# A decoder layer's tail: the last two gate tiles passed over by token halves, the sample rows turned at once

## What is computed

```
e = _rmsnorm(p_l @ w_ple, g_ple)
h = h + jax.nn.sigmoid(h @ w_ple_gate) * e
...
return _rmsnorm(h, g_final), jnp.stack(S_out), jnp.stack(buf_out)
```

## Time and profile before

| | us |
|---|---|
| timed runs, median of 3 (lowest, highest) | 1185.35 (1182.74, 1187.15) |
| the profiled execution, whole | 1180.84 |
| its span, first to last instruction | 1178.8 |
| mean granted TensorE clock in it | 0.995 of full |

### The profile page before, as it was taken

One profiled execution on the slowest core, in us unless ns is written; L12 is line 12 of the kernel. 1 busy time (PEld: TensorE's weight loads), 2 busy tenths in 40 slices (PEclk: granted clock), 3 DMA queues, 4 the chain that ended last, 5 costly groups with the idle time before them and its releaser, 6 DMA issues.

```text
span 1178.8 us, 30314 instructions
## 1 busy us (share of the span) xinstructions
PE 1163.9 (99%) x12182; PEld 1038.8 (88%) x12182; DVE 978.5 (83%) x1509; ACT 562.6 (48%) x804; POOL 55.5 (5%) x80
## 2 busy tenths in 40 slices
PE   9999999999999999999999999999999999999996
PEld 7888888888888899899998999999889999999885
DVE  6688599678867898998989989788897888887686
ACT  6445645555446744444434444444444444445442
POOL 2122210100000200000000000000000000000000
PEclk9999999999999999999999999999999999999998
DMA  7776775765566566666666666666666666667552
GB/s 257 242 231 178 233 213 180 226 181 189 175 219 197 179 213 198 201 193 201 205 212 196 195 199 195 213 208 196 196 209 189 206 205 198 196 197 249 166 158 74
DMA packets 193112, 234.89 MB, mean 199 GB/s; under 512 B 7987, under 2 KB 153626, under 8 KB 192761
## 3 DMA queue, kind: packets, MB, share of 16 engines
q1 hardware_dynamic: 187568, 220.29, 59.4%
q0 software_dynamic: 3968, 11.89, 3.5%
q10 hardware_dynamic: 1504, 1.70, 0.4%
HBM read 226.89 MB, written 7.43 MB: 199 GB/s over the span
## 4 chain that ended last, share of the span: by engine, by line
PE 90%; DVE 6%; ACT 2%; issue 1%; DMA 1%; ACTq 0%; SPq 0%; DVEq 0%
PE acc L2210 13%; PE acc L1816 10%; PE acc L1820 10%; PE acc L1818 10%; PE acc L2246 7%; PE acc L2212 6%; PE acc L2213 6%; PE acc L2191 5%; PE acc L2193 5%; PE wrk L2191 4%; PE wrk L2193 4%; PE acc L2248 4%; PE acc L2249 4%; DVE hl L952 2%; ACT hl L592 1%
## 5 line engine op out<-in xcount | busy, mean ns | idle before, releaser
L952 DVE SCALAR_TENSOR_TENSOR hl<-raw,hl 128x1024 f16<-128x1024 f32 x414 | 494.4, 1220 | 67.2 <-ACT hl L592 64.0
L592 ACT ACTIVATE hl<-raw 128x1024 f16<-128x1024 f32 x414 | 421.7, 1051 | 173.9 <-DMA raw<-in_w_down_dram 86.1
L2210 PE MATMUL acc<-nrm,hl 128*128 128x264 f16 x1344 | 274.8, 276 | 0.0
L1818 PE MATMUL acc<-nrm,hl 128*128 128x264 f16 x952 | 262.8, 276 | 0.0
L1820 PE MATMUL acc<-nrm,hl 128*128 128x264 f16 x952 | 262.7, 276 | 0.0
L1816 PE MATMUL acc<-nrm,hl 128*128 128x264 f16 x952 | 262.7, 276 | 0.0
L2212 PE MATMUL acc<-nrm,hl 128*128 128x264 f16 x672 | 185.5, 276 | 0.0
L2213 PE MATMUL acc<-nrm,hl 128*128 128x264 f16 x672 | 185.5, 276 | 0.0
L2246 PE MATMUL acc<-big,hl 128*128 128x264 f16 x704 | 146.2, 276 | 0.0
L2210 PEld LDWEIGHTS acc<-nrm,hl 128*128 128x128 f16 x1344 | 128.9, 98 | 17.8 <-DVE tg L1434 0.2
L1816 PEld LDWEIGHTS acc<-nrm,hl 128*128 128x128 f16 x952 | 93.3, 98 | 13.5 <-issue 0.4
(11 more groups left out here) (425 smaller groups left out, 2050.8 us busy)
## 6 DMA issues: line engine op xcount, KB each, us to landing
raw<-in_w_gate_up_dram SPq DMA_DIRECT2D x168, 512.0 KB, 4.6
raw<-in_w_down_dram SPq DMA_DIRECT2D x88, 512.0 KB, 4.8
raw<-in_w_in_dram SPq DMA_DIRECT2D x80, 512.0 KB, 4.4
raw<-in_w_out_dram SPq DMA_DIRECT2D x32, 512.0 KB, 4.8
raw<-in_w_ple_gate_dram SPq DMA_DIRECT2D x32, 512.0 KB, 5.2
state<-in_state_hgrn_dram POOLq DMA_DIRECT2D x8, 512.0 KB, 5.9
out_new_hgrn_sample_dram<-state POOLq DMA_DIRECT2D x8, 512.0 KB, 5.1
raw<-in_w_gate_up_dram SPq DMA_DIRECT2D x16, 256.0 KB, 3.3
```

What stands on the lines that cost most here:

```text
L592: nc.scalar.activation(hi[:, st.hl_slot(j, half), :], raw[:, st.raw_slot(j), :], ACT.Copy, scale=WSCALE).then_inc(hi_done, 1)
L952: stt(lo[:, st.hl_slot(j, half), :], raw[:, st.raw_slot(j), :], WSCALE, hi[:, st.hl_slot(j, half), :], ALU.mult, ALU.subtract).then_inc(lo ...
L1818: mm(out, wh, x_lo[:, kt, :], start=False, stop=False)
L2210: mm(out, wh, n_hi[:, kt, :], start=jj == 0 and kk == 0, stop=False, skip_group_check=bool(up))
```

## The change

Only the last gate group and what follows are touched. Tiles 0 and 1 stay as they were. Tiles 2 and 3 are made by `late_pass` in four passes, in this order: tile 2 and then tile 3 for columns 128 to 263 (half 1 and the sample tokens, `LATE_COLS`), then both for columns 0 to 127 (`LAST_COLS`), each pass over the same two weight blocks with 48 matmuls; the last two use the banks of tiles 0 and 1. Each pass has its own sigmoid (`late_sigmoid`) and VectorE steps (`late_tile`, `late_gain`), and each half its own sum of squares, root and scaling ("ya" and "yb", `late_rstd`, `scaled`). The third woven set stands in the first pass; half 1's sums and transposes ("ya", "yp_3_1") and the sample transpose are woven into the third pass behind 30 matmuls, two transposes of half 0 into the fourth. Half 1 is stored by SyncE in two DMAs of 512 KB, the sample rows behind them; half 0 in two of 384 KB by SyncE and one of 256 KB by ScalarE.

The sample rows are no longer turned tile by tile. `gained` leaves them out; one VectorE operation writes all 16 tiles' sample columns times gain into `h_smp` as 128 columns (8 tokens by 16 tiles), one transpose ("yq") turns them, and the store writes 128 rows of 512 bytes. Their squares are spread to the same 128 columns (`smp_sums`), so that one matmul gives the sum for each row. The split of block 7 moves ahead of the second `y_taken` on both engines.

```diff
-    JOBS += [(f"yp_{_c}_0", "dve"), (f"yp_{_c}_1", "act"), (f"yq_{_c}", "dve")]
-JOBS += [("ya", "dve"), ("ys", "dve"), ("yp_3_0", "dve"), ("yp_3_1", "act"), ("yq_3", "act")]
-Y_LATE, Y_CUT = 12 * P, 6 * P
+    JOBS += [(f"yp_{_c}_0", "dve"), (f"yp_{_c}_1", "act")]
+JOBS += [("ya", "dve"), ("yp_3_1", "act"), ("yq", "act"), ("yb", "dve"), ("yp_3_0", "act")]
+Y_LATE, Y_CUT, Y_EARLY = 12 * P, 6 * P, 8 * P
+LATE_TILES = (2, 3)
+LATE_COLS, LAST_COLS = slice(P, TOK), slice(0, P)
+SUMS_BEHIND, LAST_TURNS_BEHIND = 30, 8
...
+            sp.wait_ge(y_scaled, 1)
+            sp.dma_start(io["y_prompt"][0, P:SEQ, 0:Y_EARLY], y_tok[:, 1, 0:Y_EARLY]).then_inc(stored, 16)
+            sp.wait_ge(y_scaled, 2)
+            sp.wait_ge(drained["act"], drain_of("yp_3_1")[1])
+            sp.dma_start(io["y_prompt"][0, P:SEQ, Y_EARLY:], y_tok[:, 1, Y_EARLY:]).then_inc(stored, 16)
+            sp.wait_ge(drained["act"], drain_of("yq")[1])
+            sp.dma_start(io["y_sample"].rearrange("b o (k d) -> (b o k) d", d=P), y_smp).then_inc(stored, 16)
+            for n, cols in enumerate((slice(0, Y_CUT), slice(Y_CUT, Y_LATE))):
+                sp.wait_ge(y_scaled, 3 + n)
                 sp.dma_start(io["y_prompt"][0, 0:P, cols], y_tok[:, 0, cols]).then_inc(stored, 16)
-            sp.wait_ge(y_scaled_dve, 3)
...
+            def late_sigmoid(n, cols, value):
+                act.wait_ge(tail_acc, value)
+                src = acc[:, late_bank(n, cols), cols]
+                nc.scalar.activation(gate_t[:, n, cols], src, ACT.Sigmoid, scale=C_H).then_inc(tail_sig, 1)
...
+            split(S_GATE, last, 7)
             y_taken(1)
             gates(S_GATE, last, (1,), C_H, reuse=True)
-            split(S_GATE, last, 7)
             y_taken(2)
-            gates(S_GATE, last, (2, 3), C_H, reuse=True)
+            late_sigmoid(2, LATE_COLS, 1)
+            late_sigmoid(3, LATE_COLS, 2)
             act.wait_ge(mean_ready, 6)
-            nc.scalar.activation(rs[:], rs[:], ACT.Sqrt).then_inc(rstd_ready, 1)
+            nc.scalar.activation(rs[:, 1:3], rs[:, 1:3], ACT.Sqrt).then_inc(rstd_ready, 1)
+            late_sigmoid(2, LAST_COLS, 3)
...
+            nc.scalar.activation(y_tok[:, 1, Y_LATE:], y_bank(act, "yp_3_1"), ACT.Copy, scale=rs[:, 1:2])\
                 .then_inc(drained["act"], 1)
+            nc.scalar.activation(y_smp, y_bank(act, "yq")[:, 0:P], ACT.Copy, scale=rs[:, 2:3]).then_inc(drained["act"], 1)
+            late_sigmoid(3, LAST_COLS, 4)
+            act.wait_ge(mean_ready, 7)
+            nc.scalar.activation(rs[:, 0:1], rs[:, 0:1], ACT.Sqrt).then_inc(rstd_ready, 1)
+            act.wait_ge(rs_final, 2)
+            nc.scalar.activation(y_tok[:, 0, Y_LATE:], y_bank(act, "yp_3_0"), ACT.Copy, scale=rs[:, 0:1])\
+                .then_inc(drained["act"], 1)
+            act.wait_ge(drained["act"], drain_of("yp_3_0")[1])
+            act.dma_start(io["y_prompt"][0, 0:P, Y_LATE:], y_tok[:, 0, Y_LATE:]).then_inc(stored, 16)
...
-                    h = tile_of(h_all, i, n)
+                    h = tile_of(h_all, i, n)[:, 0:SEQ]
...
-                drain(nc.vector.tensor_copy(y_smp[:, y_cols(c)], y_bank(dve, f"yq_{c}")[0:NSAMP, 0:n]), f"yq_{c}")
...
+            def late_tile(n, cols, sig, at, summed):
+                dve.wait_ge(tail_sig, sig)
+                h, t, sq = tile_of(h_all, last_gate, n)[:, cols], tg32[:, 0, cols], h_sq[:, cols]
+                stt(t, gate_t[:, n, cols], one(g_ple, last_gate, n), tile_of(e_all, last_gate, n)[:, cols],
+                    ALU.mult, ALU.mult).then_inc(tail_chain, 1)
+                dve.wait_ge(tail_chain, at + 1)
+                tt(h, h, t, ALU.add).then_inc(tail_chain, 1)
+                dve.wait_ge(tail_chain, at + 2)
+                tt(sq, h, h, ALU.mult).then_inc(tail_chain, 1)
+                if summed:
+                    dve.wait_ge(tail_chain, at + 3)
+                    tt(h_ssq[:, cols], h_ssq[:, cols], sq, ALU.add).then_inc(tail_chain, 1)
...
+            def late_gain(n, toks):
+                h = tile_of(h_all, last_gate, n)[:, toks]
+                ts(h, h, one(g_fin, last_gate, n), None, ALU.mult).then_inc(hg_part, 1)
...
+            def late_rstd(name, at, n, cols, value):
+                v, r = ss[:, cols], rs[:, cols]
+                wait_job(name)
+                link(drain(ts(v, bank(name)[:, 0:n], 1.0 / D, EPS, ALU.mult, ALU.add), name))
+                nc.vector.reciprocal(r, v).then_inc(mean_ready, 1)
+                dve.wait_ge(rstd_ready, at)
+                newton(r, v, rt[:, 0:n]).then_inc(rs_final, 1)
+                dve.wait_ge(rs_final, value)
+            def scaled(a, cols):
+                ts(y_tok[:, a, cols], y_tok[:, a, cols], rs[:, a:a + 1], None, ALU.mult).then_inc(y_scaled, 1)
...
+            split(S_GATE, last_gate, 7)
             gained(last_gate, (0,))
             y_taken(1)
             gate_tile(last_gate, 1)
-            split(S_GATE, last_gate, 7)
...
+            dve.wait_ge(gate_chain, (last_gate * TPG + 2) * 3)
+            late_tile(2, LATE_COLS, 1, 0, True)
+            late_tile(3, LATE_COLS, 2, 4, False)
+            dve.wait_ge(tail_chain, 7)
+            both = [x[:, SEQ:TOK].unsqueeze(2).to_broadcast([P, NSAMP, KT]) for x in (h_ssq, h_sq)]
+            tt(smp_sums.rearrange("p (b k) -> p b k", k=KT), both[0], both[1], ALU.add).then_inc(tail_chain, 1)
+            late_gain(2, slice(P, SEQ))
+            dve.wait_ge(tail_chain, 6)
+            late_gain(3, slice(P, SEQ))
+            tt(h_smp.rearrange("p (b k) -> p b k", k=KT), h_all[:, :, SEQ:TOK].rearrange("p k b -> p b k"),
+               g_fin.unsqueeze(1).to_broadcast([P, NSAMP, KT]), ALU.mult).then_inc(hg_part, 1)
+            late_rstd("ya", 7, 2, slice(1, 3), 1)
+            dve.wait_ge(drained["act"], drain_of("yp_2_1")[1])
+            scaled(1, slice(0, Y_EARLY))
+            scaled(1, slice(Y_EARLY, Y_LATE))
+            late_tile(2, LAST_COLS, 3, 8, True)
+            late_gain(2, LAST_COLS)
+            late_tile(3, LAST_COLS, 4, 12, False)
+            late_gain(3, LAST_COLS)
+            late_rstd("yb", 8, 1, slice(0, 1), 2)
+            dve.wait_ge(drained["dve"], drain_of("yp_2_0")[1])
+            scaled(0, slice(0, Y_CUT))
+            scaled(0, slice(Y_CUT, Y_LATE))
...
                         yield
-                out = job(f"yq_{c}")
-                for n, k in enumerate(ks):
-                    last = nc.tensor.transpose(out[0:NSAMP, n * P:(n + 1) * P], h_all[:, k, SEQ:TOK], ident[:])
-                last.then_inc(job_done, 1)
-                yield
...
+            last_gate = S_GATE.groups - 1
+            stream(S_GATE, last_gate, n_hi, n_lo, sigmoid_frees=True, blocks=2 * LATE_TILES[0],
                    woven=lambda j: y_transposes(Y_AT.index(j)) if j in Y_AT else iter(()))
...
+            def late_pass(n, cols, small):
+                out = acc[:, late_bank(n, cols), cols]
+                pe.wait_ge(gate_ready, SIG_GATE + last_gate * TPG + (n + 1 - TPG if cols is LATE_COLS else n - 1))
+                for j in (2 * n, 2 * n + 1):
+                    pe.wait_ge(lo_done, S_GATE.block(last_gate, j) + 1)
+                    for kk in range(8):
...
+                        mm(out, wh, n_hi[:, kt, cols], start=begin, stop=False)
+                        next(small, None)
+                        mm(out, wh, n_lo[:, kt, cols], start=False, stop=False)
+                        next(small, None)
+                        last = mm(out, wl, n_hi[:, kt, cols], start=False, stop=end)
+                        if not end:
+                            next(small, None)
+                last.then_inc(tail_acc, 1)
+                for _ in small:
+                    pass
...
+            def late_sums():
+                out = job("ya")
+                pe.wait_ge(tail_chain, 8)
+                for src in (h_ssq, h_sq):
+                    mm(out[:, 0:1], src[:, P:SEQ], ones[:, 0:1], start=src is h_ssq, stop=src is h_sq)
+                mm(out[:, 1:2], smp_sums, ones[:, 0:1], start=True, stop=True).then_inc(job_done, 1)
+                yield
+                out = job("yp_3_1")
+                for n, k in enumerate(range(12, 16)):
+                    if k >= 14:
+                        pe.wait_ge(hg_part, k - 13)
+                    last = nc.tensor.transpose(out[:, n * P:(n + 1) * P], h_all[:, k, P:SEQ], ident[:])
+                    if k == 15:
+                        last.then_inc(job_done, 1)
+                    yield
+                pe.wait_ge(hg_part, 3)
+                nc.tensor.transpose(job("yq")[:, 0:P], h_smp, ident[:]).then_inc(job_done, 1)
+                yield
+            late_pass(2, LATE_COLS, y_transposes(2))
+            late_pass(3, LATE_COLS, iter(()))
+            late_pass(2, LAST_COLS, behind(SUMS_BEHIND, late_sums()))
+            sums, turns = job("yb"), job("yp_3_0")
...
+            pe.wait_ge(hg_ready, KT - 2)
+            late_pass(3, LAST_COLS, behind(LAST_TURNS_BEHIND, last_turns((12, 13))))
```

(59 more changed lines are left out.)

55 lines of the change are left out of this document (7 added, 48 removed).

## The result

| | before | after |
|---|---|---|
| timed runs, median (lowest to highest), us | 1182.74 (1181.27 to 1187.15), 7 runs | 1176.97 (1176.42 to 1178.87), 7 runs |
| the profiled execution, whole / span, us | 1180.84 / 1178.8 | 1178.87 / 1177.1 |
| start of the last gate group to the span's end ("the tail" from here on), us | 38.76 | 34.68 |

The ratio is 0.9949, with an interval of 0.9933 to 0.9964: the changed kernel is faster by about half a per cent, 6 us, where 2.8 were forecast. The time lies under the range. A span is listed to 0.1 us, so a tail is good to 0.05.

What follows compares the result with a forecast made beforehand. TensorE, busy 99% of the span, was taken as the bound, then a latency chain and stores. TensorE +1.0 us, first issue 0.12 earlier, and stores 2.7 us instead of 5.5 gave -2.8: 1182.5 us, range 1179.5 to 1186.0.

Steps and rivals of the forecast that it cites:

- What follows the data stays: 1.5 to the landing and 0.6 to the end.: Kernel's end, after the last store's data: landing and closing keep their 1.5 and 0.6 us.
- The prediction's first rival: Kernel's end: the landing comes 0.55 us sooner, transposes cost 0.11, no stall; gain 4.3 us, time 1181.0, chance 0.15.
- I take the difference to the median: 1185.35 - 2.8 = 1182.5: Whole kernel: the 2.8 us gain is subtracted from the median of three timed runs, 1185.35 us.
- rival of exposed weight loads: Four late passes: weight loads not overlapped make short matmuls 7.7 us dearer, +4.9 net, 1190.3 us; chance 0.06.
- Woven transposes: TensorE's late passes: seven moved transposes at 0.16 us add 1.12; eight of the third woven set add 0.40.
- The sums of "ya": Three sum matmuls moved into TensorE's stream, 0.105 us each, adding 0.32 us.
- The stall: TensorE's wait before "ya" for VectorE's eighth tail step: 0.2 us, bounds 0 to 0.8.
- The chain: After the last accumulating matmul: sigmoid, VectorE steps, sum and root for 128 tokens; first issue at 1170.45, 0.12 us earlier.
- The table loads: ScalarE: two more loads of 1.28 us, both hidden, the second by 0.3; rival has them exposed, 1183.8 us, chance 0.08.
- half 1 is not out before half 0: Final stores: 2.1 MB queue at the end again, only 0.12 us gained, 1185.2 us; chance 0.03.
- The TensorE queue gives it back: TensorE's late passes: transposes at 0.22 and a 0.8 us wait before "ya" add 1.5 us, 1184.0; chance 0.18.
- Larger gain: Kernel's end and TensorE: sooner landing, transposes at 0.11, no stall; gain 4.3 us, time 1181.0, chance 0.15.

Runs made afterwards that it cites:

- e4: Kernel before without the store of the sample rows (y_sample not written), against the kernel before: ratio 0.9984, time -1.7 us, tail 37.53 us.
- e6: Changed kernel with its sample store issued last and in 8 rows instead of 128; ratio to the kernel before 0.9973, tail 35.59 us.
- e9: Kernel before without the three woven sample transposes and their copies, sample store as 128 rows; ratio to before 0.9969, tail 36.30 us.
- e2: The changed kernel run again unchanged, beside the kernel before: ratio 0.9965, time -3.3 us, tail 34.64 us.
- e7: Kernel before without the three woven sets of sample transposes and their copies: ratio to before 0.9979, time -1.7 us, tail 37.36 us.
- e8: Changed kernel with half 1's sums behind 36 matmuls of the third pass instead of 30; ratio to the kernel before 0.9952, tail 34.33 us.
- e3: Changed kernel with half 1's and the sample stores held until half 0's first piece is scaled; ratio to before 0.9991, tail 37.44 us.
- e1: The kernel before, unchanged, timed against itself: ratio 0.9997, time +0.2 us, tail 38.73 us.

## Why the prediction was wrong

Tail by tail, the forecast against what the traces show (each row ends where the next begins):

| stretch | before | forecast | after |
|---|---|---|---|
| last gate group on TensorE | 25.59 | 26.6 | 26.25 |
| its end to the first issue of the last stores | 4.94 | 3.81 | 3.85 |
| first issue to the end of the stream | 6.13 | 3.45 | 3.53 |
| end of the stream to the end of the span | 2.10 | 2.10 | 1.05 |
| sum | 38.76 | 36.0 | 34.68 |

**The step that failed.** "What follows the data stays: 1.5 to the landing and 0.6 to the end." It did not stay: it fell to 1.05, and this is most of the 1.3 us by which the sum missed. I had read the 2.1 us as the fixed price of a DMA's end, because the DMA rate drops at 1176.7. It was the sample store, whose rows were still on their way until 1177.82; e4, e6 and e9 show that shape to cost 1.0, 0.8 and 1.1. The trace of before held the evidence: the view of its DMA queues from 1176.5 to 1177 has

```profile
q1 hardware_dynamic: 7, 0.06, 89.1%
```

so seven packets of SyncE's queue that start there take 7.1 us together. The change list held the mechanism: "the store writes 128 rows of 512 bytes" was described, and never costed. The prediction's first rival did doubt the 1.5 ("a 256 KB store lands 2.4 us after its issue"), but it found 0.55 of the 1.05 us and gave no mechanism, and it had a chance of 0.15. The Trainium skill has a rule on it ("DMA: Bandwidth & Descriptors", Why a DMA increments its semaphore by 16 and not by 1, the part on how many engines): a DMA is dealt to the largest number of engines up to 16 that divides its slowest dimension on both sides. By it the 8 rows go to 8 engines and the 128 rows to all 16. The trace agrees as far as it goes: eight packets in flight behind the stream, where the stream had 16; which engine a packet is on it doesn't say. Why a row takes 1.05 us stays open. At the pace of the 5 KB pieces of the prompt stores (0.20 us each) it would be 0.33, and it is not the size of the packet alone: the 256 packets of 8 KB that load data in the kernel's first 9 us, on the same queue, have a median of 0.32. No run here separates the eight partitions, the direction and the length of a row.

**The starting point.** The second thing that failed, and the larger in the time, was the base: "I take the difference to the median: 1185.35 - 2.8 = 1182.5". Three runs were too few; the medians of before, over 7 to 28 runs, are 1182.74, 1182.06, 1182.19 and 1182.94. Of the 5.5 us between 1182.5 and 1176.97, 2.6 are this base, 1.3 the tail, and the remaining 1.6 I put down to the scatter of the front in the first comparison (e2 has the same kernel at 1178.72). So the base counts for more than the landing in the time's fall below the range: from 1182.74 the forecast gain gives 1179.9, and the tail's gain 1178.6. The forecast for the profiled execution itself was 1178.0; with the tail as it was it would have been 1176.8.

**TensorE, +0.66 instead of +1.0.** Near as a total, by terms that partly cancel:
- Sample transposes: 1.37 removed, 1.32 forecast (e7).
- Short matmuls: 96 x 0.0591 + 96 x 0.0560 = 11.05 against 10.79, so 0.26 for 0.29. The rival of exposed weight loads is out. So is, for this stream, the 0.081 us per 128-column matmul of the Trainium skill ("TensorE: Matmul & The Clock Gate", Back-to-back issue gap): thirty in a row here are 0.056 apart, and eighty of 136 columns 0.059, at a granted clock of 1.00.
- Woven transposes: four of them with the matmul between span 0.68 us (1164.29 to the fifth at 1164.97), so 0.17 - 0.056 = 0.114 each and not 0.16. Seven cost 0.80 for 1.12, and the third set next to nothing for 0.40. A weight load of 0.141 did not show behind a 0.056 matmul.
- The sums of "ya": 0.66 for 0.32. The mis-sizing is in the count. I read "x6" as six matmuls of 0.105; here the two sums of `h_ssq` and `h_sq` are listed as x4 and the third as x2. So a sum in f32 is listed as two instructions and costs 0.22.
- The stall: 0.28 for 0.20, in its bounds (e8).

These add to -1.37 + 0.26 + 0.80 + 0.66 + 0.28 = 0.63 of the 0.66 measured.

**The chain** was forecast within 0.04 us, in part by luck. The sigmoid and VectorE's three steps took 1.51 for 1.59; the way to TensorE and back 0.48 for 0.36, by the same miscount of the sums ("One matmul in place of six", where it was one of three); the root 1.21 and the issue 0.65, as forecast.

**The table loads** cost nothing in the tail, but not quite by the cover that was forecast. After's last group starts 2.38 us later than before's, so its times are set back by that to meet the prediction's. The sigmoid's load was to be over at 1163.95, with its pass; it was over at 1163.92 (1166.30). But the pass had ended at 1163.43 (about 1165.81: eight matmuls of 0.056 before the fourth pass's first transpose at 1166.26), so the sigmoid waited some 0.3 us for its table; the fourth pass ran until 1168.67 and hid it. The last root came 0.60 after its load was over (1169.17 + 1.28 = 1170.45, against 1171.05), where 0.3 of cover was forecast. That rival is out, and the 1380 ns of drain that it cites are not in this trace: the sigmoid starts 0.02 us after its load is over (1165.02 + 1.28 = 1166.30, against 1166.32).

**The other rivals.** The stores of half 1 are worth 2.76 us against 2.8 (e3); "half 1 is not out before half 0" is out with it. *The TensorE queue gives it back* happened in the small, the 0.28 of the stall. *Larger gain* comes near in its number, 4.3 us against the 4.1 of the tail, but partly by luck. It was right on the transposes (0.114 for its 0.11). It had half of the landing (0.55 of 1.05), no stall where there was one of 0.28, and the sums 0.34 too cheap like the forecast; the first of these errors offsets the other two. Net of the 1.32 of the sample transposes, the forecast gave the passing over by halves 1.5 us, and e9 leaves 1.6 for it: what was missed of the tail is mostly the shape of the store.

The chances of 0.90 for no change that can be told and 0.07 for faster rested on the true gain. A gain of 4.1 us is 0.35%, inside the 0.5% bound; the first comparison has 0.51%, hardly beyond it.

## What to carry to other kernels

At the end of a kernel, look at the DMA traffic of the last three microseconds at the finest scale, and ask for each packet after the stream whose it is, and when it ends: "landing time" may be a small store of few long rows. Here 128 short rows came with turning all sample rows at once, at no price that the runs show. Cost also what a change lists as a mere consequence of its layout: the store's shape, which had no term in the forecast, brought 1.06 of the 4.1 us, and all that was done to the sample rows 2.4, more than the passing over by halves. Time a kernel more than three times before a forecast is counted from it: this base was 2.6 us off. And compare a stretch with a stretch: the tail repeated within 0.04 us where the whole kernel scatters by 4.

## What was not expected of the hardware

- Eight packets of 8 KB, one for each sample row, took 1.05 us each on average at the end of before, and were alone in flight for 0.5 us, where the stream of 390 GB/s had 16; the last ended 1.06 us after the stream had. The same 64 KB as 128 rows came through right behind the stream (e9), at 0.027 us a row.
- 8 KB packets are not slow as such: 256 of them at the kernel's start have a median of 0.32 us.
- From the end of the last data packet to the end of the span it is 0.91 us before and 0.90 after, whichever store is last, and 0.74 (e9) to 0.96 (e1) in all twelve traces: there is no fixed price of 2 us behind the data.
- f16 matmuls of 128 columns with weights of their own run 0.056 us apart, and f32 transposes of 128 columns between them take 0.114, though the weight load of such a transpose is listed with 0.141.
- A sum over partitions with a column of ones costs 0.22 us on TensorE in f32, as much as two transposes (2 x 0.114), though it has one column.
